# Taking out the twelve products of ones by ones ahead of the first weight unit

## The reference

```
h = rms_norm(x, norm_g);  z = h @ w_in          # 1024 -> 9 groups of columns
y_rnn = (rg_lru(x_rnn, ...) * silu(g_rnn)) @ rg_out
y_sc  = (sc_b * conv(sc_c * x_sc) * silu(g_sc)) @ sc_out
y_att = (mla(c_q, c_kv, k_rope, ...) * silu(g_att)) @ mla_out
merged = gates[0]*y_rnn + gates[1]*y_sc + gates[2]*y_att
x = x + merged @ w_out                          # per layer; meta rows dropped at the end
```

## Time and profile before

| | us |
|---|---|
| median of 3 runs (lowest, highest) | 1672.87 (1672.76, 1673.4) |
| the profiled execution | 1674.52 |
| its span, first to last instruction | 1672.7 |
| TensorE busy in it | 1663.2 (99%) |
| POOL busy | 1257.1 (75%) |
| VectorE busy | 1157.2 (69%) |
| ScalarE busy | 600.9 (36%) |

### The profile page before, as it was taken

How to read it: one execution, slowest core, us unless ns; L and a number is a source line. 1 busy time by engine, 2 the same in 40 slices (tenths; PEclk the granted TensorE clock), 3 DMA queues, 4 the chain that set the end, 5 groups by cost and what they waited for, 6 DMA issues and landing times.

```text
span 1672.7 us, 32259 instructions
## 1 busy us (share of the span) xinstructions
PE 1663.2 (99%) x11912; PEld 1566.6 (94%) x11912; DVE 1157.2 (69%) x1622; ACT 600.9 (36%) x1073; POOL 1257.1 (75%) x1334
## 2 busy tenths in 40 slices
PE   9999999999999999999999999999999999999999
PEld 8999999999999999999998888888888888999887
DVE  7966758485677778776349657484847887778751
ACT  5523333242344344432135233332323434444320
POOL 7774848385899869897866748483868997899983
PEclk9999999999999999999999999999999999999999
DMA  4432223222333243432532313232323334333333
GB/s 164 142 100 64 94 62 93 68 82 93 104 107 101 101 141 115 125 116 76 167 119 77 112 60 97 63 92 68 93 86 106 101 113 141 114 127 127 113 101 116
DMA packets 52746, 173.19 MB, mean 104 GB/s; under 512 B 6544, under 2 KB 7952, under 8 KB 52624
## 3 DMA queue, kind: packets, MB, share of 16 engines
q1 hardware_dynamic: 44352, 153.04, 28.9%
q10 hardware_dynamic: 8320, 19.17, 3.3%
HBM read 156.53 MB, written 15.14 MB: 103 GB/s over the span
## 4 chain that ended last, share of the span: by engine, by line
PE 88%; DVE 7%; issue 2%; ACT 1%; DMA 0%; ACTq 0%; DVEq 0%; SPq 0%; POOL 0%; POOLq 0%
PE slots L656 65%; PE slots L940 13%; PE slots L721 3%; PE slots L755 3%; PE slots L739 1%; PE slots L828 1%; DVE early L1591 1%; DVE early L1606 1%; DVE qr_hi_and_lo L1418 1%; DVE kr_lo L1418 1%; DVE kn_lo L1418 1%; PE slots L690 1%; PE slots L706 0%; DMA residual_or_merged<-xt 0%; DVE early L1613 0%
## 5 line engine op out<-in xcount | busy, mean ns | idle before, releaser
L525 POOL TENSOR_TENSOR w_lo<-w_raw,w_hi 128x256 fp32r<-128x256 f32 x828 | 737.7, 920 | 17.3
L520 POOL TENSOR_SCALAR w_hi<-w_raw 128x1024 fp32r<-128x1024 f32 x207 | 251.7, 1216 | 206.4 <-PE slots L656 191.7
L656 PE MATMUL slots<-h_hi,w_hi 128*128 128x264 f32 (+1 forms) x1584 | 379.7, 307 | 0.9 <-DVE sc_pad L1719 0.9
L656 PE MATMUL slots<-h_lo,w_hi 128*128 128x264 f32 (+1 forms) x1584 | 374.2, 304 | 0.0
L656 PE MATMUL slots<-h_hi,w_lo 128*128 128x264 f32 (+1 forms) x1584 | 373.9, 303 | 0.0
L656 PEld LDWEIGHTS slots<-h_hi,w_hi 128*128 128x128 f32 x1584 | 255.0, 188 | 13.7 <-issue 2.0
L656 PEld LDWEIGHTS slots<-h_hi,w_lo 128*128 128x128 f32 x1584 | 254.2, 188 | 11.6
L656 PEld LDWEIGHTS slots<-h_lo,w_hi 128*128 128x128 f32 x1584 | 254.4, 188 | 10.7
L595 POOL TENSOR_TENSOR w_lo<-w_raw,w_hi 128x256 fp32r<-128x256 f32 x132 | 126.0, 986 | 43.5 <-ACT w_hi L1329 43.5
L656 PE MATMUL slots<-branch_hi,w_hi 128*128 128x264 f32 (+1 forms) x552 | 143.4, 319 | 2.0 <-DVE branch_lo L1431 2.0
L656 PE MATMUL slots<-branch_lo,w_hi 128*128 128x264 f32 (+1 forms) x552 | 141.5, 315 | 0.0
(11 more groups left out here) (279 smaller groups left out, 3796.0 us busy)
## 6 DMA issues: line engine op xcount, KB each, us to landing
w_raw<-w_units SPq DMA_DIRECT2D x251, 512.0 KB, 3.6
stream<-sc_acc ACTq DMA_DIRECT2D x16, 264.0 KB, 2.1
stream<-h_blend ACTq DMA_DIRECT2D x8, 528.0 KB, 2.7
h_mixes<-stream SPq DMA_DIRECT2D x8, 528.0 KB, 4.6
sc_back<-stream SPq DMA_DIRECT2D x8, 528.0 KB, 3.7
x_old<-stream SPq DMA_DIRECT2D x16, 264.0 KB, 4.6
stream<-residual_or_merged ACTq DMA_DIRECT2D x16, 264.0 KB, 2.9
ab_raw<-w_units SPq DMA_DIRECT2D x8, 512.0 KB, 4.3
```

What stands on the lines that cost most here:

```text
L520: pool.tensor_scalar(hi, raw, 1.0, 1.0, ALU.mult, ALU.mult).then_inc(sem("hi_part"), 1)
L525: op = pool.tensor_tensor(lo[:, cols], raw[:, cols], hi[:, cols].bitcast(F32), ALU.subtract)
L656: mm = pe.matmul(out[:, a_, 0:t1 - t0], w(k), x(k)[:, t0:t1], start=(n == 0), stop=(n == 3 * ks - 1))
```

## The change

The wait for the fill of `ones`, the wait for slot 3 and the twelve matmuls are taken out. Nothing else differs: the fill of `ones` stays, and so does every later wait.

```diff
@@ -767,11 +767,6 @@
                     dense("CQ", l, 0, name, j, xg_hi, xg_lo, lambda k: at("xg_lo", l, 0, k + 1),
                           l == DEPTH - 1 and name[0] == "q", ks)
 
-                if l == 0:
-                    pe.wait_ge(sem("made"), 1)
-                    pe.wait_ge(*slot_free("NORM", l, 0, "stat"))
-                    for _ in range(12):
-                        pe.matmul(ps[:, 3, 1, 0:P], ones[:], ones[:], start=True, stop=True)
                 latent("kv0", 0)
                 latent("kv1", 1)
                 latent("q0", 2, range(0, 4))
```

## The result

The changed kernel takes 1678.23 us (median of 7 runs, 1677.7 to 1679.96), the kernel before beside it 1672.87 (7 runs, 1672.56 to 1674.34). The ratio is 1.0031, with a 95% interval of 1.0022 to 1.0041. It is slower by 5.4 us, where no change was forecast and the range ended at 1675.8.

The account below looks back on a forecast made before the run. The arrival of x and its split bound the start, TensorE everything from 15.73 us on. Work 0, clock 0 and code 0 left 1674.52 us profiled, less 1.65 to the median: 1672.9 us, range of 8 in 10 1672.0 to 1675.8.

Parts of the forecast that it names:

- The part removed, as work: At 1.64 to 6.89 us: the twelve products, 5.25 us of TensorE work beside the transfer of x, worth 0.
- The part removed, as warming: At the start: without the twelve, TensorE's low clock reaches into real products; worth 0 to +3.6 us, taken as 0.
- the rise at 12.7: In the first unit: the clock rises 5.8 us after the first product at 6.9, at a cost of 0.
- the 14.3 that would have cost time: In the first unit: a clock rise up to 14.3 us is free, a later one costs half of its lateness.
- The sign that the forecast had named, an eighth tile later than 15.8: First unit's last tile: expected within 0.1 us of 15.73; a start later than 15.8 would make the forecast wrong.
- The rival of the late clock: At 6.9 to 21.5 us: the clock rises after 14.3, costing 2.8 to 3.6 us, giving 1676.1; chance 0.15.
- The part moved: TensorE's code ahead of the first loop gets shorter, loop bodies keep their place; 0, bounds -0.3 and +2.5 us.
- its rival at 0.03: At the loop's entry: code falls badly on its blocks, one wait up to 2.5 us, giving 1674.3; chance 0.03.
- Its own sign, a gap ahead of the loop's first product: At the loop's entry: a gap there would show the step on moved code, taken as 0, to be wrong.
- The rival's size: At the loop's entry: up to 2.5 us of wait, 1.1 hidden by ScalarE's later start, so 1.4 us; chance 0.03.
- The bound: For the moved code: +2.5 us, the longest wait without a shown cause anywhere in the chain.

Follow-up runs that it names:

- e1: Changed kernel plus 98 waits met at once (49 instructions) where the twelve products stood, code as long as before; 1674.18 us, ratio 1.0002 to the kernel before.
- e4: Changed kernel with the loop's first instruction pinned to slot 64 of a block instead of 0; 1674.11 us, ratio 1.0001 to the kernel before.
- e7: Changed kernel plus 74 waits met at once (37 instructions) in place of the products; 1674.05 us, ratio 0.9999 to the kernel before.
- e3: Changed kernel plus 26 waits met at once (13 instructions) in place of the products; 1679.49 us, ratio 1.0033 to the kernel before.
- e6: Changed kernel plus 50 waits met at once (25 instructions); six runs at 1673.81 to 1674.39 us, four at 1678.45 to 1679.98.
- e2: Kernel before with three products of 512 columns in place of the twelve of 128, 13 instructions longer than the changed kernel; 1679.49 us, ratio 1.0032.
- e8: Changed kernel without head_slot, so nothing is pinned and the loop follows its entry directly; 1674.01 us, ratio 0.9999 to the kernel before.
- e12: Changed kernel with the loop's first instruction pinned to slot 16 of a block instead of 0; 1674.13 us, ratio 1.0001 to the kernel before.
- e9: Changed kernel plus three unread 512-column products straight ahead of the loop, waiting for nobody (12 instructions); 1677.26 us, ratio 1.0019 to the kernel before.
- e5: Changed kernel plus three unread 512-column products ahead of the loop, in slot 3 behind a wait until it is free; 1681.83 us over four runs.
- e11: Changed kernel without the hi by lo products of units kv1 and q1 of the first layer, 64 instructions shorter; 1674.27 us.

## Why the prediction was wrong

- **The part removed, as work: 0.** Held. The first real product of e1, e4 and e7 starts at 6.8 to 6.9 as before (the 7.43 of the changed kernel's profile is alone among the twelve without the products), and e1 is within 0.2 us of before without the twelve.
- **The part removed, as warming: 0, with the rise at 12.7.** Held, the size of the delay by luck. The rise came at 13.3, 5.9 us after the first product, where 5.8 was assumed. But in e3 and e6, which start the same way, the products are fast from 10.7 and 10.2 on, 3.6 and 3.2 us after the first, so the delay is not a constant of the kernel; all rises lie ahead of the 14.3 that would have cost time. A slow product cost 0.22 and not 0.244 us, which was one of the two values weighed. The eighth tile started 0.13 us behind its remainder (15.95, 16.08). e2 against e3, 0.0 us apart, prices this warming at nothing. The sign that the forecast had named, an eighth tile later than 15.8, is there in the changed kernel's profile (16.08), but for the later landing of x and not for the clock. The rival of the late clock gave a time of 1676.1, the nearest to the result of all; its mechanism had no part in it.
- **The part moved: 0, with bounds of -0.3 and +2.5 us.** This is the step that failed, with its rival at 0.03. Its own sign, a gap ahead of the loop's first product, is in the profile (3.02 us idle). It read: "The loop's first instruction is pinned to slot 0 of a block by the code itself (L813), so the loop bodies and what follows keep their place in a block". That is true and beside the point: pinning the target does not pin the branch ahead of it, and where the branch lies against its target decides (e1 moves the one, e4, e8 and e12 the other; either takes the stall away). The pin is even what made the stall possible, since e8 without it and e12 and e4 with another slot have none.
- **The rival's size.** It was priced at 2.5 us less 1.1 hidden behind ScalarE, 1.4 us. The stall was 3.16 us, next to nothing of it was hidden (e9, which has the stall alone, is 3.1 us above before), and it drew 2.0 us of low clock behind it. I had weighed the clock only where products were taken away, at the start, and never asked of a stall later in the kernel whether TensorE's rest would lower the clock as well. The bound was an idle time on VectorE's chain, the nearest row there was; no row of before shows TensorE at a branch whose target is missing.
- **Where it could have been seen.** The dense stretch at the loop's entry shows only that the old placement was a good one. The instruction packets of the queues, at 48.75 and 53.5, were in the trace of before, and the prediction made no use of them. They would have hinted at it: a packet came 4.4 us ahead of the loop's first product, with 36 products and 36 weight loads between, and 49 instructions were to be taken out.

## What to carry to other kernels

An edit that changes the number of instructions ahead of a large loop also moves the branch into it against the blocks in which code is fetched. Before its time is put down to what the edit does, run one version with the same count of harmless instructions in its place, or with the head at another slot; and look in the profile for the instruction packets of the DMA queues near each loop's entry. If TensorE must rest there, the low clock afterwards costs again: here 3.1 us of stall became 5.4 us.

## What had not been expected of the hardware

- The wait for a missing block of code cost TensorE 3.16 us (idle for 3.02 to 3.33 us in the four profiles with a stall and no filler), and the array goes on with what has been issued meanwhile (e9: 2.82 us of products in 3.29 us).
- The clock did not fall at the end of the rest but early in it. TensorE's last token sum ends at 53.63 in the changed kernel, and the granted clock drops 0.7 us later; it is back at 61.1, 4.5 us after work had begun again (stretches of the changed kernel, columns as above):

```profile
54.20:54.30 0.10, 0.00 (x0) 0.00 (x0) 0.10 (x1) 0.00 (x0) 0.10 (x2) 1.00 0.89 211
54.30:54.40 0.10, 0.00 (x0) 0.00 (x0) 0.10 (x1) 0.00 (x0) 0.10 (x1) 0.60 0.69 169
```

  In e3 it drops at 55.0, 1.7 us into the rest. In the profiled execution of e5 a rest of 1.80 us did not lower it, nor did one of 0.47 us in e9. So the length of the rest alone does not tell whether the clock falls.
- The clock can fall without any long rest. In e11 no idle time of TensorE between 24 and 52 us is over 0.57 us, and yet its products at the loop's entry are 0.213 us apart and the stretch from 52 to 56 us has a granted clock of 0.57. TensorE in e11:

```profile
47.30 1.06 PE L795 MATMUL slots<-ones,early 128*106 128x1 f32 x10 [0.57 <-DVE early L1480]
...
50.42 1.16 PE L710 MATMUL slots<-residual_or_merged,ones 64*128 64x264 f32 x4 [0.49 <-DVE lane_consts L1539]
51.51 1.10 PE L795 MATMUL slots<-ones,early 128*106 128x1 f32 x10
52.47 0.53 PE L827 MATMUL slots<-w_hi,kv_hi 128*106 128x256 f32 x1
52.80 0.41 PE L827 MATMUL slots<-w_lo,kv_hi 128*106 128x256 f32 x1
53.01 0.41 PE L827 MATMUL slots<-w_hi,kv_lo 128*106 128x256 f32 x1
```

  The mean granted clock orders the ten executions of e11: 1673.3 to 1673.8 us at 1.0, 1676.6 and 1676.9 at 0.998, and 1673.3 to 1675.2 at 0.999. What lowered it there, the short idle times or the token sums of one column each, stays open; these sums stand ahead of the rest in the changed kernel too. It also stays open where exactly the blocks lie: the trace shows when a packet goes, not which instruction it brings.
- The granted clock of the profile shows the fall at 54.3 us (0.60, then 0.50) but not the low level at the start, where it says 1.00 beside products that are 0.22 us apart. At the start only the distance of the products tells it.
